# Pooling, convolution taps and the last projection units rescheduled in a two-block fp32 transformer kernel

## The reference

```python
# block 1: gated linear attention in both directions, a pooling branch
o, _, _ = gla_bidir(q, k, v, la_f, la_b, s_f, s_b, True)
o_n = rmsnorm(o, gla_norm_g)              # over each head's 256 values
yA = (o_n * silu(zA)) @ w_branch_a
yB = (multiscale_pool(uB, w_pool, pool_scale) * silu(zB)) @ w_branch_b
x = x + gate * ((sigmoid(gA) * yA + sigmoid(gB) * yB) @ w_out)
# pool: centred averages of 2, 4, 8, 16 tokens, one window for each quarter
# of the channels, less the input; then a 256 x 256 product for each quarter
x = rmsnorm(x, final_norm_g)
# block 2
z = modulate(rmsnorm(x)) @ w_in
att = neighbourhood_attention(q, k, v, k_ctx, v_ctx, rpb)   # 8 heads of 64
u, v = gelu(z_u), layernorm(gelu(z_v))
sg = u * (w_s @ v + b_s)                  # over chunks of 128 tokens
h = dwconv31(a * sigmoid(gate)) + b       # 31 taps, 256 channels
cv = silu(group_layernorm(h))
x = x + gate * (concat(att, sg, cv) @ w_out)
x = x + gate2 * conv_ffn(modulate(rmsnorm(x)))
out = rmsnorm(x, final_norm_g_2)
```

## Time and profile before

| | before |
|---|---|
| median of 3 runs | 2660.3 us (2650.6 to 2660.5) |
| profiled execution: time | 2659.43 us |
| profiled execution: span | 2657.6 us |
| mean granted clock of TensorE, of full speed | 0.966 |
| VectorE busy | 1516.2 us (57%) |
| GpSimd busy | 1057.7 us (40%) |
| ScalarE busy | 731.2 us (28%) |
| shares of the chain that ended last | PE 50%, DVE 8%, issue 3%, ACT 1%, DMA 1% |

### The profile page before, as it was taken

One profiled execution on the slowest core, in us unless ns is written; L12 is line 12 of the kernel. 1 busy time (PEld: TensorE's weight loads), 2 busy tenths in 40 slices (PEclk: granted clock), 3 DMA queues, 4 the chain that ended last, 5 costly groups with the idle time before them and its releaser, 6 DMA issues.

```text
span 2657.6 us, 33035 instructions
## 1 busy us (share of the span) xinstructions
PE 2493.3 (94%) x12008; PEld 2042.5 (77%) x12008; DVE 1516.2 (57%) x2193; ACT 731.2 (28%) x1244; POOL 1057.7 (40%) x493
## 2 busy tenths in 40 slices
PE   8999999999999889999986999899799999999997
PEld 4888788888887768877765887677578888888885
DVE  5796156878511466537796544465864444444446
ACT  4411334444200354123232444432211111111112
POOL 2344333333376524467540111025554444444444
PEclk9999999999999989999996899899899999999998
DMA  9576455444576632434211223421111111111111
GB/s 353 183 252 247 146 166 153 151 155 151 196 274 253 258 140 95 140 111 133 89 54 44 80 70 89 152 86 56 57 56 47 47 48 48 47 47 47 47 47 72
DMA packets 131090, 324.72 MB, mean 122 GB/s; under 512 B 11553, under 2 KB 59233, under 8 KB 125473
## 3 DMA queue, kind: packets, MB, share of 16 engines
q1 hardware_dynamic: 91376, 215.90, 24.9%
q10 hardware_dynamic: 39600, 107.30, 11.3%
HBM read 248.04 MB, written 70.39 MB: 120 GB/s over the span
## 4 chain that ended last, share of the span: by engine, by line
PE 50%; DVE 8%; issue 3%; ACT 1%; DMA 1%; DVEq 0%; POOL 0%; SPq 0%; ACTq 0%
PE pb L483 36%; PE g L2994 6%; PE g L3067 2%; PE pb L2994 1%; DVE zcs L2261 1%; PE g L3047 1%; PE g L2975 1%; DVE f_spare L2470 1%; PE g L2854 1%; DVE xl L2173 1%; DMA kept_in<-cs_d 1%; PE g L2973 0%; DVE ml L2477 0%; DVE hl L2540 0%; DVE cb L2519 0%
## 5 line engine op out<-in xcount | busy, mean ns | idle before, releaser
L851 POOL TENSOR_TENSOR w_hi<-w_raw,one 128x1024 fp32r<-128x1024 f32 x191 | 398.8, 2088 | 1461.3 <-PE pb L483 1062.7
L854 POOL TENSOR_TENSOR w_lo<-w_raw,w_hi 128x1024 fp32r<-128x1024 f32 x191 | 516.2, 2703 | 14.9
L483 PE MATMUL pb<-xh,w_hi 128*128 128x512 f32 (+1 forms) x1224 | 474.8, 388 | 18.8 <-DVE zkr L2232 8.8
L483 PE MATMUL pb<-xh,w_lo 128*128 128x512 f32 (+1 forms) x1224 | 467.2, 382 | 0.0
L483 PE MATMUL pb<-xl,w_hi 128*128 128x512 f32 (+1 forms) x1224 | 467.0, 382 | 0.0
L483 PE MATMUL pb<-mh,w_hi 128*128 128x512 f32 x704 | 279.0, 396 | 16.0 <-DVE ml L2477 7.3
L483 PEld LDWEIGHTS pb<-xh,w_hi 128*128 128x128 f32 x1224 | 233.1, 190 | 66.9 <-issue 9.4
L483 PE MATMUL pb<-mh,w_lo 128*128 128x512 f32 x704 | 276.5, 393 | 0.0
L483 PE MATMUL pb<-ml,w_hi 128*128 128x512 f32 x704 | 276.1, 392 | 0.0
L483 PEld LDWEIGHTS pb<-xl,w_hi 128*128 128x128 f32 x1224 | 232.6, 190 | 44.2
L483 PEld LDWEIGHTS pb<-xh,w_lo 128*128 128x128 f32 x1224 | 233.1, 190 | 42.8 <-issue 0.7
(11 more groups left out here) (414 smaller groups left out, 4632.2 us busy)
## 6 DMA issues: line engine op xcount, KB each, us to landing
w_raw<-in_wall SPq DMA_DIRECT2D x190, 512.0 KB, 3.6
mod_later<-in_modw SPq DMA_DIRECT2D x28, 1024.0 KB, 6.2
proj_d<-stage ACTq DMA_DIRECT2D x40, 512.0 KB, 3.0
at_bias<-in_bias SPq DMA_DIRECT2D x64, 192.0 KB, 2.8
mod_raw<-in_modt SPq DMA_DIRECT2D x8, 1024.0 KB, 10.6
w_raw<-in_wall ACTq DMA_DIRECT2D x15, 512.0 KB, 6.5
svt<-vt_d ACTq DMA_DIRECT2D x11, 512.0 KB, 6.3
vc<-proj_d SPq DMA_DIRECT2D x10, 512.0 KB, 6.1
```

The lines of the kernel that those rows point to most:

```text
L483: mm = pe.matmul(pb[bank][:, 0:n], w[:, b, wc:wc + P], x[:, k, tokens], start=(count == 0), stop=(count == total - 1))
L851: nc.gpsimd.tensor_tensor(w_hi[:, b, :], w_raw[:, b, :], one[:, 0:1].to_broadcast([P, 1024]), ALU.mult).then_inc(w_high, 1)
L854: nc.gpsimd.tensor_tensor(w_lo[:, b, :], w_raw[:, b, :], w_hi[:, b, :], ALU.subtract).then_inc(w_split, 1)
```

## The change

It has three independent parts.

**Pooling.** The barrier at the end of phase 4 goes for ScalarE, VectorE and TensorE; TensorE waits for the eighth eviction (`f_oev` 8) instead. ScalarE makes the high parts of group 0 behind chunk 4 of the forward pass and the first two silus behind chunk 5 (`q_silu`, now a function apart from `q_gate`); VectorE makes the low parts of group 0 behind chunk 5. `dl` holds all eight tiles, in the place of `qd`; `dh` has two buffers at new addresses. The square of head 0 comes behind the high parts of group 1, into a buffer of its own (`osq_first`), and TensorE takes `o_means(0)` between groups 0 and 1. VectorE takes the low parts of group n + 2 behind the gate of group n.

**Convolution.** The running sum of the taps lies in banks 0 to 3 of `g` (`conv_sum`); the last tap of each tile reads it there and writes `zcs`. The gating's transposes therefore use banks 4 and 5 alone, in two halves with ScalarE's copies (`gating_tokens`) between, one ahead of the first key tile and one behind it. The small products for the gating's bias (`sgw_sb`) move ahead of the gating's projections. ScalarE makes all eight high parts of the context behind the first gating unit instead of three, three and two; VectorE takes their low parts ahead of the taps. Its small operations and low parts stand at other taps than before; the mean that ScalarE's squares of the gating wait for (`y_dve` 2) comes behind tap 19.

**Attention.** In steps 32 to 41 lie the last eight projection units: the two context units (256 tokens) in one step each, six others in two steps each. Before, they took steps 32 to 43. `r1` is loaded at step 35 and its reciprocal taken in quarters in steps 37 to 40; `kept_in` is loaded at step 41, and steps 44 to 47 take one operand each. The load of `x2` is cut in two, and the second part (tiles 2 to 7) is waited for only at the output units of tile 2 on. The three heads move to steps 55 to 57.

The diff, cut to its core (counts of semaphores that only shift are left out):

```diff
+dh = [at("dh0", [P, 2, T], arena + 136 * 1024, F32R)[0], at("dh1", [P, 2, T], arena + 149 * 1024, F32R)[0]]
...
+dl, _ = at("dl", [P, 8, T], arena, F32R)
...
-dh, a = at("dh", [P, 2, 2, T], a, F32R)
-dl, a = at("dl", [P, 2, 2, T], a, F32R)
+osq_first, _ = at("osq_first", [P, 2, T], arena + 160 * 1024)
...
-KEPT_AT = ((0,), (1,), (2, 3))
+KEPT_AT = {44: (0,), 45: (1,), 46: (2,), 47: (3,)}
+HEADS_AT = {55: 0, 56: 1, 57: 2}
...
-        return W2_FIRST + k, "W", 3, k, 0
-    n = k // 2
-    if i == 2 and n >= 6:
-        return None
+        return W2_FIRST + k, "W", 3, k, range(4, KT)
+    n, ks = k // 2, (range(0, 4), range(4, 8))[k % 2]
+    if i == 2:
+        if k >= 10:
+            return None
+        n, ks = (k, range(KT)) if k < 2 else ((k + 2) // 2, ks)
     kind, part = (("K", 2), ("V", 2), ("V", 0), ("V", 1), ("Q", 0), ("Q", 1), ("K", 0), ("K", 1))[n]
-    return 8 * i + n, kind, i + 1 + n // 6, part, k % 2
+    return 8 * i + n, kind, i + 1 + n // 6, part, ks
...
-        if s == 44:
-            sp.wait_ge(d_done, W2_FIRST)
+        if s == 35:
             sp.wait_ge(kept_out, 96)
             sp.wait_ge(at_kd, 128)
-            sp.dma_start(r1[:, :], r1_d).then_inc(kept_back, 16)
+            sp.dma_start(r1[:, :], r1_d).then_inc(sg_in, 16)
+        if s == 41:
+            sp.wait_ge(d_done, W2_FIRST)
             sp.dma_start(kept_in[:, :, :], cs_d.rearrange("t p n -> p t n")).then_inc(kept_back, 16)
         if s == 46:
             sp.wait_ge(at_s, 48)
-            sp.dma_start(x2[:, :, :], xp_d.rearrange("t p n -> p t n")).then_inc(x2_in, 16)
+            for begin, end in ((0, 2), (2, KT)):
+                sp.dma_start(x2[:, begin:end, :], xp_d[begin:end].rearrange("t p n -> p t n"))\
+                  .then_inc(sg_in if begin else x2_in, 16)
...
+    def q_high(grp):
+        if grp >= 2:
+            act.wait_ge(unit_done, UNIT[T_POOL] + 4 * grp - 4)
+        act.wait_ge(q_in[grp], 16)
+        for n in (2 * grp, 2 * grp + 1):
+            act.activation(dh[grp % 2][:, n % 2, :], qd[:, n, :], ACT.Copy).then_inc(q_dh, 1)
+    def q_silu(grp):
+        for n in (2 * grp, 2 * grp + 1):
+            act.wait_ge(q_z[n % 2], 16 * (n // 2 + 1))
+            act.activation(zb[:, n % 2, :], zb[:, n % 2, :], ACT.Silu).then_inc(q_sil, 1)
...
-    end_phase(act, 4)
...
+        if c == 4:
+            q_high(0)
+        if c == 5:
+            q_silu(0)
...
-    act.wait_ge(u_d, 17)
-    q_high(0)
-    for grp in range(1, 4):
-        q_high(grp)
-        q_gate(grp - 1)
...
+    act.wait_ge(u_d, 17)
+    q_high(1)
+    act.wait_ge(f_oev, NCX + 1)
+    o_squares(0, osq_first)
+    for grp in range(3):
+        q_gate(grp)
+        if grp < 2:
+            q_high(grp + 2)
+        q_silu(grp + 1)
+    act.wait_ge(unit_done, UNIT[T_POOL] + 4)
     o_load_za(0)
     q_gate(3)
-    o_squares(0)
...
-        for k in (3 * t, 3 * t + 1, 3 * t + 2):
-            if k < KT:
-                act.wait_ge(t_ready, 5 * KT + k + 1)
-                act.activation(xh[:, k, T:TA], ctx_raw[:, k, :], ACT.Identity,
-                               bias=modc[:, 24 + k:25 + k]).then_inc(xh_ready, 1)
+        for k in range(KT) if t == 0 else ():
...
+    gating_tokens(0)
+    for n in range(3):
+        pair_k_high(0, n, pair_unit(u_k + n))
+    gating_tokens(4)
+    act.wait_ge(y_dve, 2)
...
-        if s == 45:
-            act.wait_ge(kept_back, 128)
-        for j in KEPT_AT[s - 45] if 45 <= s < 48 else ():
+        if s == 44:
+            act.wait_ge(kept_back, 112)
+        for j in KEPT_AT.get(s, ()):
             operand_high(4 + j, kept_in[:, j, :])
-        if 52 <= s < 55:
-            if s == 52:
-                act.wait_ge(kept_back, 144)
-            operand_high(s - 52, heads_in[:, s - 52, :])
+        if s in HEADS_AT:
+            if HEADS_AT[s] == 0:
+                act.wait_ge(kept_back, 128)
+            operand_high(HEADS_AT[s], heads_in[:, HEADS_AT[s], :])
...
-    end_phase(dve, 4)
...
+        if c == 5:
+            q_low(0)
...
-    q_low(0)
-    for grp in range(1, 4):
-        q_low(grp)
-        q_gate(grp - 1)
-    q_gate(3)
+    dve.wait_ge(u_d, 17)
+    q_low(1)
+    for grp in range(4):
+        if grp == 1:
+            for n in range(U_BUFS):
+                dve.wait_ge(u_out[n], 64)
+        q_gate(grp)
+        if grp < 2:
+            q_low(grp + 2)
...
+    def conv_sum(t):
+        return g[:, 2 * t:2 * t + 2, :].rearrange("p a n -> p (a n)")
...
                 dve.wait_ge(z_cv, tap * 2 + (t - 1))
                 nc.vector.scalar_tensor_tensor(
-                    zcs[:, t, :], hpad[:, t, bass.ds(tap, T)],
+                    conv_sum(t), hpad[:, t, bass.ds(tap, T)],
                     col[:, bass.ds(tap + (cw + TAPS * t), 1)],
-                    zcs[:, t, :], ALU.mult, ALU.add).then_inc(z_cv, 1)
+                    conv_sum(t), ALU.mult, ALU.add).then_inc(z_cv, 1)
...
-    taps(1, 5)
     for k in range(KT):
         ctx_low(k)
-    taps(5, 14)
-    nc.vector.tensor_scalar(vstat[:, 3, 0:2], col[:, COL["sg_b"]:COL["sg_b"] + 2], float(C), None, ALU.mult)
-    dve.wait_ge(y_act, 1)
-    nc.vector.tensor_scalar(vstat[:, 0, :], vstat[:, 0, :], -1.0 / C, None, ALU.mult).then_inc(y_dve, 1)
-    dve.wait_ge(y_dve, 1)
     dve.wait_ge(y_pe, 1)
     for t in range(2):
-        nc.vector.scalar_tensor_tensor(sgb_sb[:, t, :], g[:, 4, P * t:P * t + P], vstat[:, 3, t:t + 1],
-                                       sgb_sb[:, t, :], ALU.mult, ALU.add)
-    for n, (first, last) in enumerate(((14, 17), (17, 18), (18, 20))):
+        v = nc.vector.scalar_tensor_tensor(sgb_sb[:, t, :], g[:, 4, P * t:P * t + P], vstat[:, 3, t:t + 1],
+                                           sgb_sb[:, t, :], ALU.mult, ALU.add)
+    v.then_inc(y_dve, 1)
+    taps(1, 15)
+    for n, (first, last) in enumerate(((15, 17), (17, 18), (18, 20))):
         pair_k_low(0, n, pb[(u_k + n) % 2], bank_free[(u_k + n) % 2])
         taps(first, last)
-    dve.wait_ge(y_act, 3)
+    dve.wait_ge(y_act, 2)
+    nc.vector.tensor_scalar(vstat[:, 0, :], vstat[:, 0, :], -1.0 / C, None, ALU.mult).then_inc(y_dve, 1)
+    taps(20, 24)
+    dve.wait_ge(y_act, 4)
     nc.vector.reciprocal(vstat[:, 1, :], vstat[:, 1, :]).then_inc(y_dve, 1)
-    dve.wait_ge(y_dve, 2)
+    dve.wait_ge(y_dve, 3)
     nc.vector.tensor_tensor(vstat[:, 2, :], vstat[:, 0, :], vstat[:, 1, :], ALU.mult).then_inc(y_dve, 1)
-    for n, (first, last) in enumerate(((20, 23), (23, 25))):
+    for n, (first, last) in enumerate(((24, 27), (27, 29))):
         taps(first, last)
         pair_q_low(0, n, pb[(u_q + n) % 2], bank_free[(u_q + n) % 2])
-    taps(25, TAPS)
+    taps(29, TAPS - 1)
+    for t in range(2):
+        dve.wait_ge(z_cv, 2 * TAPS - 3 + t)
+        nc.vector.scalar_tensor_tensor(
+            zcs[:, t, :], hpad[:, t, TAPS - 1:TAPS - 1 + T], col[:, cw + TAPS * t + TAPS - 1:cw + TAPS * t + TAPS],
+            conv_sum(t), ALU.mult, ALU.add).then_inc(z_cv, 1)
...
-        if s in (45, 46):
-            dve.wait_ge(kept_back, 128)
-            part = r1[:, half_of(s - 45)]
-            nc.vector.reciprocal(part, part).then_inc(rstd_ready, 1)
-        for j in KEPT_AT[s - 45] if 45 <= s < 48 else ():
-            operand_low(4 + j, kept_in[:, j, :], 5 + j)
-        if 52 <= s < 55:
-            operand_low(s - 52, heads_in[:, s - 52, :], s - 43)
+        if 37 <= s < 41:
+            if s == 37:
+                dve.wait_ge(sg_in, 48)
+            part = r1[:, C * (s - 37):C * (s - 37) + C]
+            v = nc.vector.reciprocal(part, part)
+            if s % 2 == 0:
+                v.then_inc(rstd_ready, 1)
+        for j in KEPT_AT.get(s, ()):
+            operand_low(4 + j, kept_in[:, j, :], 6 + j)
+        if s in HEADS_AT:
+            operand_low(HEADS_AT[s], heads_in[:, HEADS_AT[s], :], 10 + HEADS_AT[s])
...
-    end_phase(pe, 4)
+    pe.wait_ge(f_oev, 8)
...
+        if grp == 1:
+            o_means(0, osq_first)
...
-    o_means(0)
...
+    pe.wait_ge(sg_in, 32)
+    for q in range(4):
+        t, r = q // 2, 64 * (q % 2)
+        mm = pe.matmul(g[r:r + 64, 4, P * t:P * t + P], mean_v[:, 0:64], sgw_sb[:, q, :], start=True,
+                       stop=True)
+    mm.then_inc(y_pe, 1)
...
     evicted(pe, UNIT[T_PAIR])
-    pe.wait_ge(sg_in, 32)
-    for q in range(4):
-        t, r = q // 2, 64 * (q % 2)
-        mm = pe.matmul(g[r:r + 64, 4, P * t:P * t + P], mean_v[:, 0:64], sgw_sb[:, q, :], start=True,
-                       stop=True)
-    mm.then_inc(y_pe, 1)
-    for n in range(NCX):
-        for t in range(2):
-            o = (2 * n + t) * P
-            mm = pe.transpose(g[:, o // H, o % H:o % H + P], zcs[:, 6 + t, CH * n:CH * n + CH], ident)
-    mm.then_inc(y_pe, 1)
+    pe.wait_ge(y_dve, 1)
+    gating_transposes(0)
     pe.wait_ge(xl_ready, 6 * KT)
     pe.wait_ge(xh_ready, 6 * KT)
     pe_tile(pe, T_PAIR)
+    pe.wait_ge(y_act, 1)
+    gating_transposes(4)
     pe_tile(pe, T_PAIR + 1)
     pe_tile(pe, T_PAIR + 2)
```

(1 more changed line is left out.)

131 lines of the change are left out of this document (67 added, 64 removed).

## The result

The changed kernel took 2621.2 us (median of 4 runs, 2620.0 to 2624.7) beside 2655.5 us for the kernel before (2644.7 to 2660.5): the ratio is 0.9878, with a 95% interval of 0.9842 to 0.9915. Measured again, on another chip beside the experiments, it took 2620.1 beside 2650.1, ratio 0.9885 (0.9868 to 0.9903). So it is faster by about 30 us, 1.2%; the first pair of medians is 34.2 us apart, on four runs each. The prediction said 2629 for 2621.2, a gain of 30.8 us.

A forecast was written before the change was run, and what follows sets the result against it. TensorE, busy 94% of the span, was taken as the bound, so gains come only where it waits or its clock is down. Pooling -8, taps -17.8, attention -4, heads -1 sum to -30.8, giving 2629 us; range 2612 to 2647.

The forecast's parts named there:

- The new wait for the value unit: Convolution stage: ScalarE's squares and root hold back the first value unit's eviction, so TensorE waits 4 us, at no cost.
- the wait for the tap: End of the convolution: TensorE's wait for the last tap becomes 8 to 11 us instead of 18.4.
- The same-bank rival: Taps: reading and writing one PSUM bank costs 1.05 us more a tap, 63 us in all; time 2692; chance 6%.
- The collisions: Taps beside GpSimd weight splits: collisions cost 14.7 us; rival that they stay gives 2644, chance 5%.
- the split: Pooling: making tiles 0 and 1 during forward chunks 4 and 5 gives only 2.3 us.
- VectorE paces what follows: Pooling behind the forward pass: VectorE sets the pace, 1.67 us a half tile, about 7.5 us a group.
- The 6.7 us behind the last low part: Pooling end: head 0's square and eight products move amid the groups, saving 6.7 us before the first branch unit.
- Two context steps: Attention from step 32: the two context units, in one step each, take 12.4 us for two steps.
- the load: Attention: loading 2 MB of kept_in takes some 8 us and is waited for by perhaps 2 us (0 to 5).
- Steps 34 to 41: Attention: eight steps behind the context units stay at 45.0 us, plus 1.75 for the reciprocal quarter in step 39.
- All goes through: Whole kernel, rival: the clock holds after shorter waits and the load is in time; 2614 us; chance 12%.
- only the taps gain: Whole kernel, rival: the attention's and pooling's gains are eaten by the clock and VectorE's pace; 2642 us; chance 13%.

The follow-up runs named there:

- the kernel with the first group late: Changed kernel with group 0's high parts, silus and low parts behind chunk 7 of the forward pass instead of amid chunks 4 and 5; 2630.9 us.
- the products last: Changed kernel with o_means(0) behind the last pooling group, as before the change, its squares still made early; 2617.7 us.
- the squares last too: Kernel with o_means(0) behind the last group, its squares also made there, behind ScalarE's part of group 3; 2628.5 us.

## Why the prediction came out as it did

- **The level.** The prediction started from the profiled execution (2659.4) and a median of three runs (2660.3), two of which lie in the range of the upper group. The kernel's median over 25 executions is 2651.0. The sum of the terms, -30.8, is within a microsecond of what the medians give (-30.0 to -30.5); the 8 us between 2629 and 2621 are the base. The long stretch at the low clock in steps 0 to 4 stood in the earlier trace rows, and the prediction took it for a trait of the kernel.
- **Taps: right, term by term.** A median of 1282 ns was measured for 1.20 us a tap in a row (1.19 in 33.45 us for 28) and 1.27 to 1.30 us long. The last one ends at 1384.8; the prediction's 1394, less the 9.3 us that the pooling had gained, is 1384.7. The lead from the stage is 17.7 for 17.8. The new wait for the value unit is 3.4 for "4", the wait for the tap 8.2 for "8 to 11". The same-bank rival is out: reading and writing one bank costs 7 ns a tap more than SBUF (1275 ns). The Trainium skill's 65 ns for a PSUM source (VectorE: DVE Perf Modes, TRN2 errata) isn't borne out by the same 7 ns. The collisions went, as the Trainium skill has it (SBUF — State Buffer, Who interferes with whom); the Trainium skill gives the cause, the runs give its size: 1.89 us or 32.18 for one conversion.
- **Pooling: right size (8.0 for 8), one step mis-sized.** The prediction gave the split 2.3 us, with the last low part at 945.4. It came at 942.6, though the forward pass ended 0.9 us later: 6.0 us earlier in all. That is one execution: behind the last forward product the last low part ends at 42.6 to 45.7 us in the eight profiles with this pooling, and at 46.6 to 48.6 in the three without it, 4.4 us apart by the means. The step that was mis-sized is "VectorE paces what follows": TensorE's wait at the start, with the low clock behind it, went through the whole train, as the kernel with the first group late shows. The 6.7 us behind the last low part went nearly whole (0.4 us are left), but what brought it is the early square, not the place of the products: 0.3 us with the products last, 6.5 with the squares last too. What was given back is the clock of the first branch products, 0.63 us each.
- **Steps 32 to 48: a sum that held by luck, from parts that didn't.** Two context steps 12.1 for 12.4, steps 42 and 43 7.2 for 7.2, the load 7.8 us for 8. Steps 34 to 41 took 50.1 for 46.75: the reciprocal in step 39 was found and priced at its own 1.75 us, and the clock behind it was left out. Steps 44 to 47 took 21.2 for 25, since `kept_in` had landed (1668.2) before step 44 needed it; step 48 took 10.8 for 7.5, at the low clock. The sum is 101.3 for 98.9 and 102.4 before, so in these profiles the steps gained 1.1 of the forecast 3.5 (in that of the attention part alone, 99.0 us, with 9.7 for step 40). By medians this part with the heads gives 3.6 for 5, in an interval from a loss of 1.6 to a gain of 7.
- **The chances.** "All goes through" (2614) is nearer to 2621 than "only the taps gain" (2642), but not because the clock held: in the last steps it fell as the forecast had it.

## What to carry to other kernels

Price a step from the trace, but take the level from many executions: a stage at the low clock may belong to the execution and not to the kernel. A short instruction that delays TensorE costs its own time and what the clock takes behind it, here 4.8 us of a step (11.3 for 6.5) and 4.1 by the medians, for 1.75. When VectorE works beside GpSimd for long, let it read one operand from PSUM. And fill a wait of TensorE with no more than it holds: one unit of 5.4 us in a wait of 8.2 gained here, two (with other edits) did not.

## What the runs showed of the chip that was not expected

- A row of 28 VectorE instructions with both inputs in SBUF held one GpSimd instruction for 32.18 us, while they themselves ran at 1.20 us each. With the running sum in PSUM, in and out, neither engine lost anything (1282 ns, 1.89 us).
- One program had executions about 9 us apart, 36 and 11 of 47, with nothing between. The profiled ones at the upper end have a stretch of 41.0 us at half the clock at one place, and others do not; that it makes the two groups is read from this and not shown. It began 24 us after another low stretch had ended, that of an 18 us wait. Behind a wait of 8.2 us both profiles of the changed kernel are without it, and none of its 9 times looks like it.
